# Residual and norm vectors loaded during the recurrence, query turns waiting bank by bank, in a two-block transformer kernel on one core

## The reference

```python
# block 1, MLA
q = (_rmsnorm(c_q, q_norm) @ w_uq).reshape(B, L, MLA_HEADS, MLA_QK_DIM)
q = jnp.concatenate([q[..., :MLA_NOPE_DIM], _rope(q[..., MLA_NOPE_DIM:], cos, sin)], axis=-1)
k = jnp.concatenate([k_nope, jnp.broadcast_to(k_rope, (B, L, MLA_HEADS, MLA_ROPE_DIM))], axis=-1)
mla = _block_sweep(q, k, mv, MLA_QK_DIM ** -0.5, key_end, mla_mask)
# block 2
...
x = layer_norm_affine(ALPHA * x + gt1 * mix_l, ln1_g, ln1_b)
h2 = modulate(layer_norm(x), sh2, sc2)
logits = jnp.einsum('btd,de->bte', h2, router_w)
ffn_l = expert_choice_ffn(h2, router_w, w_gate, w_up, w_down)
x = layer_norm_affine(ALPHA * x + gt2 * ffn_l, ln2_g, ln2_b)
```

## Time and profile before

| what | value |
|---|---|
| median of 3 runs | 1576.49 us (1571.98 to 1577.51) |
| the profiled execution, its own time | 1569.62 us |
| its span, first to last instruction | 1567.5 us |
| TensorE busy | 1427.5 us, 91% of the span, mean granted clock 0.959 |
| VectorE, ScalarE, GpSimd busy | 49%, 26%, 13% |
| DMA | 284.99 MB, mean 182 GB/s |
| chain that ended last | PE 75%, issue 10%, DVE 8%, ACT 2%, DMA 2%, POOL 2% |

### The profile page before, as it was taken

The page is one execution under the profiler, slowest core; times in us unless marked ns, Lnnn a source line. Parts: engine busy times, 40 slices in busy tenths (PEclk is TensorE's granted clock), DMA queues, the critical chain, the costliest instruction groups (busy, mean ns, idle before and its releaser), DMA issues.

```text
span 1567.5 us, 31894 instructions
## 1 busy us (share of the span) xinstructions
PE 1427.5 (91%) x14033; PEld 821.8 (52%) x14033; DVE 762.7 (49%) x1437; ACT 404.9 (26%) x902; POOL 206.6 (13%) x220
## 2 busy tenths in 40 slices
PE   7999999999999999969999997884999898998986
PEld 4546576764645556757888885352333332332322
DVE  5987455455236646656667765464132132122124
ACT  3220154632100025544555543011100000000002
POOL 1200013100001110033344362011000000000000
PEclk9999999999999998989999998895999999999998
DMA  7575321401401111000000000734999999999992
GB/s 283 194 255 195 142 107 31 149 1 41 176 27 54 54 54 55 1 2 4 5 4 4 4 4 26 326 126 176 394 428 426 427 427 429 427 426 429 428 428 102
DMA packets 50730, 284.99 MB, mean 182 GB/s; under 512 B 3992, under 2 KB 7320, under 8 KB 37792
## 3 DMA queue, kind: packets, MB, share of 16 engines
q1 hardware_dynamic: 46736, 267.20, 42.3%
q0 software_dynamic: 2704, 10.18, 1.9%
q10 hardware_dynamic: 1152, 5.57, 0.9%
HBM read 276.63 MB, written 6.29 MB: 180 GB/s over the span
## 4 chain that ended last, share of the span: by engine, by line
PE 75%; issue 10%; DVE 8%; ACT 2%; DMA 2%; POOL 2%; ACTq 0%; DVEq 0%; SPq 0%; POOLq 0%
PE PS L1319 15%; PE PS L1105 7%; PE PS L1339 7%; PE PS L723 7%; PE PS L1635 4%; PE PS L588 3%; PE PS L569 3%; PE PS L1123 3%; PE PS L553 3%; PE PS L1357 3%; PE PS L1702 2%; PE PS L691 2%; PE PS L685 2%; PE PS L759 2%; PE PS L547 2%
## 5 line engine op out<-in xcount | busy, mean ns | idle before, releaser
L1319 PE MATMUL PS<-arena 128*64 128x512 f32 x304 | 141.3, 615 | 14.9 <-issue 14.9
L1321 PE MATMUL PS<-arena 128*64 128x512 f32 x304 | 141.4, 615 | 0.0
L771 PE MATMUL PS<-arena,ring 128*128 128x512 f32 (+1 forms) x368 | 127.6, 508 | 0.0
L1319 PE MATMUL PS<-ring,arena 128*64 128x512 f32 x208 | 99.7, 630 | 12.5 <-issue 11.5
L723 PE MATMUL PS<-ring,arena 128*128 128x512 f32 (+1 forms) x256 | 109.1, 583 | 1.9 <-ACT arena L1769 1.9
L1105 PE MATMUL PS<-arena 64*64 64x64 f32 x3776 | 92.5, 224 | 9.5 <-DVE arena L1418 3.9
L771 PEld LDWEIGHTS PS<-arena,ring 128*128 128x128 f32 x368 | 69.4, 189 | 58.2 <-issue 54.3
L1321 PE MATMUL PS<-ring,arena 128*64 128x512 f32 x208 | 99.8, 631 | 0.0
L2479 DVE TENSOR_TENSOR arena<-PS,arena 64x512 f32<-64x512 f32 x32 | 22.1, 689 | 157.9 <-PE PS L1341 157.6
L645 DVE TENSOR_REDUCE arena<-PS 128x1 f32<-128x768 f32 (+4 forms) x96 | 62.7, 655 | 74.2 <-PE PS L553 25.5
L1319 PEld LDWEIGHTS PS<-arena 128*64 128x64 f32 x304 | 41.4, 141 | 101.7 <-issue 100.9
(11 more groups left out here) (382 smaller groups left out, 2683.3 us busy)
## 6 DMA issues: line engine op xcount, KB each, us to landing
arena<-exp_w_down SPq DMA_DIRECT2D x20, 2048.0 KB, 36.1
arena<-exp_w_gate SPq DMA_DIRECT2D x19, 2048.0 KB, 31.5
arena<-exp_w_up SPq DMA_DIRECT2D x19, 2048.0 KB, 35.7
ring<-exp_w_gate SPq DMA_DIRECT2D x13, 2048.0 KB, 29.6
ring<-exp_w_up SPq DMA_DIRECT2D x13, 2048.0 KB, 34.1
ring<-w_ada SPq DMA_DIRECT2D x12, 2048.0 KB, 12.8
ring<-exp_w_down SPq DMA_DIRECT2D x12, 2048.0 KB, 35.0
ring<-w_in SPq DMA_DIRECT2D x9, 2048.0 KB, 7.8
```

What stands on the lines that cost most here:

```text
L771: mm = pe.matmul(bank(b, 0, n), u[:, k, (i % 4) * P:(i % 4) * P + P], hT[:, k, t0:t0 + n], start=(k == 0), stop=(k == KT - 1))
L1319: pe.matmul(bank(c, 0, 512, (0, 64)), x, unit(u)[:, k, c * 512:c * 512 + 512], start=(n == 0 and k == 0), stop=(n == 1 and k == 3))
L1321: mm = pe.matmul(bank(c, 0, 512, (64, 128)), x, unit(u + 1)[:, k, c * 512:c * 512 + 512], start=(n == 0 and k == 0), stop=(n == 1 and k == 3))
```

## The change

The residual, `ln1` and the router are loaded by SP and no longer by ScalarE. SP issues `ln1` and the router when phase 6 (GQA) is over, and the residual when all operations of the recurrence have signalled, that is during RWPOST. The lives of the three tiles begin earlier accordingly. In MLAPREP each pair of heads waits only for the job slot in which its two banks lie (`q_bank`), and VectorE copies the odd heads, ScalarE the even ones.

```diff
-    ("x2", 4 * D, OUT2, FINAL), ("ln1", 2 * D, OUT2, ROUTE),
+    ("x2", 4 * D, RWPOST, FINAL), ("ln1", 2 * D, RWKV, ROUTE),
-    ("xn", 4 * D, OUT2, ROUTE), ("h2T", 2 * D, OUT2, ROUTE), ("router", 128, OUT2, ROUTE),
+    ("xn", 4 * D, OUT2, ROUTE), ("h2T", 2 * D, OUT2, ROUTE), ("router", 128, RWKV, ROUTE),

+SCAN_TOTAL = {}
+for _name, _n in SCAN_COUNT.values():
+    SCAN_TOTAL[_name] = max(_n, SCAN_TOTAL.get(_name, 0))

@@ SP @@
                 elif slot == SCAN_SLOT:
+                    sp.wait_ge(sem("phase_left"), 4 * 6)
+                    sp.dma_start(T("ln1"), w["ln1"].broadcast_to([P, 2 * D])).then_inc(sem("ln1_loaded"), 16)
+                    sp.dma_start(T("router"), w["router_w_2"][0].rearrange("(p k) e -> p k e", k=KT))\
+                        .then_inc(sem("ln1_loaded"), 16)
+                    for name, n in SCAN_TOTAL.items():
+                        sp.wait_ge(sem(name), n)
+                    sp.dma_start(T("x2"), x1_dram).then_inc(sem("x1_back"), 16)
                     sp.wait_ge(sem("phase_left"), 4 * 7)

@@ TensorE @@
+        def q_bank(h):
+            last_four = [n for n, j in enumerate(JOBS) if j[0] == MLAPREP][-4:]
+            return 2 * slot_of(last_four[h // 2]) + h % 2

-            for n in n0[-4:]:
-                e, c = emptied(n)
-                pe.wait_ge(sem("slot_dve" if e == "d" else "slot_act"), c)
             pe.wait_ge(sem("q_roped"), 4)
             for h in range(H):
+                if h % 2 == 0:
+                    n = n0[h // 2 - 4]
+                    e, c = emptied(n)
+                    pe.wait_ge(sem("slot_dve" if e == "d" else "slot_act"), c)
                 for t in range(4):
-                    mm = pe.transpose(bank(h, t * P, P, (0, QK)), qrow[:, t, h * QK:h * QK + QK], ident)
+                    mm = pe.transpose(bank(q_bank(h), t * P, P, (0, QK)), qrow[:, t, h * QK:h * QK + QK], ident)

@@ ScalarE @@
-            for h in range(H):
+            for h in range(0, H, 2):
                 act.wait_ge(sem("q_turned"), h + 1)
-                act.activation(mqT[0:QK, h, :], bank(h, 0, 512, (0, QK)), ACT.Copy, scale=MLA_SCALE)
+                act.activation(mqT[0:QK, h, :], bank(q_bank(h), 0, 512, (0, QK)), ACT.Copy, scale=MLA_SCALE)
...
-            act.dma_start(T("x2"), x1_dram).then_inc(sem("x1_back"), 16)
-            act.dma_start(T("ln1"), w["ln1"].broadcast_to([P, 2 * D])).then_inc(sem("ln1_loaded"), 16)
-            act.dma_start(T("router"), w["router_w_2"][0].rearrange("(p k) e -> p k e", k=KT))\
-                .then_inc(sem("ln1_loaded"), 16)

@@ VectorE @@
             jobs_empty(dve, "d", MLAPREP, rope_q)
+            for h in range(1, H, 2):
+                dve.wait_ge(sem("q_turned"), h + 1)
+                dve.tensor_scalar(mqT[0:QK, h, :], bank(q_bank(h), 0, 512, (0, QK)), MLA_SCALE, None, ALU.mult)
```

## The result

The changed kernel takes **1564.52 us**, the median of 7 runs (1559.30 to 1568.14). The kernel before, run beside it, takes 1575.24 (7 runs, 1569.37 to 1577.51). The ratio is 0.9935, with a 95% interval of 0.991 to 0.9959: 10.7 us faster by the medians, with an interval that leaves out 1. One execution of one kernel further down (`logits` later), 1867.87 us at a mean granted clock of 0.74 where all others have about 0.96, is left out of that kernel's ratio.

A forecast was written before the change was run, and what follows sets the result against it. TensorE, busy 91% of the span, was taken to bound the kernel. OUT2's 7.5 us plus the query turns' 2.0 us made 9.5 us, taking the 1576.49 us median to 1567.0, range 1560 to 1574.5.

The forecast's parts named there:

- OUT2, 7.5 us: Start of OUT2: TensorE's 5.64 us idle before the first turn goes, and 1.9 us returns through the clock.
- The upper bound of 8.7: OUT2: the most it could gain, the 8.7 us by which VectorE starts earlier.
- The time of issue moves too, and that carries the 7.5.: OUT2's three loads: issuing them earlier, when DMA engines are 2% and 1% busy, brings the 7.5 us.
- a mere move to SP would leave the wait where it is: OUT2's loads: changing only the issuing engine keeps the wait, leaving just the 2.0 us of the query turns.
- The residual as the case to reckon with: OUT2: the residual, 12.7 us in the crowd, would land at about 964, 28 us before VectorE needs it.
- The turns, 2.0 us: End of MLAPREP: earlier query turns and shared copies hand over at 279.0, not 280.98; bounds 0.9 to 2.6 us.
- What is late next: OUT2 after the change: TensorE no longer waits for VectorE's tile 1 and sets the pace to the end of `mixed(3)`.
- Addresses, nothing: Arena: the three tiles' longer lives move most tiles to other addresses, taken to cost nothing.
- The signs: Expected profile after: no idle before the first turn, residual near 962, `mixed(3)` done 9.5 us earlier, MLA's first matmul at 279.0.
- Rival A: OUT2: the idle goes but the clock stays low; 6.5 to 7.6 us gained, 1569 to 1570 us; chance 0.17.
- Rival B: OUT2's loads stay in the crowd or the expert stage gives the gain back; 1574.5 us; chance 0.08.
- Rival C: Recurrence: new loads hold up instruction fetches, 20.2 us cost, 10.7 us slower overall, 1587 us; chance 0.05.

The follow-up runs named there:

- `logits` later: Changed kernel with TensorE's logits(0) moved from ahead of mixed(3) to behind turn_xn(2); ratio to the kernel before 0.9934, run again 0.9923.
- the kernel with all copies on ScalarE: Changed kernel with ScalarE copying all eight query heads again, the bank-wise waits kept; ratio to the kernel before 0.9945.
- the kernel with eight loads: Changed kernel with the 1 MB load of `ln1` repeated seven more times during the recurrence; ratio to the kernel before 0.9941.
- the run with the vectors early: Changed kernel with the residual issued by ScalarE at OUT2's start again, only `ln1` and the router loaded early; ratio to the kernel before 0.9939.
- the addresses alone: Kernel before with only the longer lives of the three tiles, giving the changed kernel's arena addresses; ratio to the kernel before 0.9989.

## Why the prediction was right, and where its reasons were not

- **The time.** 1567.0 was predicted, 1564.5 measured, inside 1560.0 to 1574.5. The sum was 9.5 us, the two stages gained 10.66, inside its bounds of 6.5 and 11.3. Both parts moved by the mechanism that the sum names: TensorE's idle time and slow clock behind it in OUT2, and its wait for all four slots ahead of the turns.
- **OUT2, 7.5 us.** Measured 8.45 in the profile of after (7.6 to 8.8 over the profiles of kernels that leave the tail of OUT2 as it is). The parts, by the rows: the idle time 5.64 as said; the turn 1.97 - 0.87 = 1.10 as said; `mixed(2)` 14.64 - 13.74 = 0.90 for 0.8. Most of the rest, 0.77, is `mixed(0)` with `mixed(1)`, 29.81 for 30.58: the first 16 us of the stage were granted 0.87 after and 0.82 before, and the sum has no term for that. Whether it belongs to the change is open: the four profiles in which ScalarE still issues the residual there have 30.54 to 30.58, the others 29.43 to 30.09, but the kernel with all copies on ScalarE, whose loads are those of the changed kernel, has 30.66. The upper bound of 8.7 held in the profile of after; the kernel with eight loads, at 8.84, goes just past it.
- **"The time of issue moves too, and that carries the 7.5."** The early issue is enough for the gain, as the profile after shows, but this step took it for the cause, and it is not needed. Issued no earlier than before, but ahead of the expert units, the loads give the same OUT2 within the spread (105.76); behind them, 122.89. What the kernels that gain have in common is that all three loads have landed when `mixed(0)` is done; in the kernel before, `ln1` and the router came behind the residual, beside the expert units. The Trainium skill, "DMA: Bandwidth & Descriptors", section "Issuing engines are not separate DMA queues", says that transfers of all issuers run on the same 16 DMA engines and interleave. The runs agree: the residual takes 12.7 and 12.9 us on ScalarE beside the units, 7.7 alone. The conclusion that I drew from it, that a mere move to SP would leave the wait where it is, came out in neither place: the router lands after 24.3 us on ScalarE beside the units, 4.8 on SP ahead of them and 26.8 behind them.
- **The residual as the case to reckon with.** The working followed its 12.7 us. Early, it took 7.7 (the estimate, 12.7, was too long), and it did not need to be early at all: the run with the vectors early shows the gain with the residual left in the crowd.
- **The turns, 2.0 us.** Measured 2.21. VectorE's copy took 0.68 us for the 0.69 assumed. The hand-over came at 284.44 - 5.67 = 278.77 on the clock of before (5.67 is how much later the projection's row stands, 276.21 for 270.54), not at 279.0: the 0.2 us that I let pass between the last turn and its copy did not show, VectorE being still at head 5 until 283.68 when the last turn was over at 283.64. The path that I gave, last turn and then its copy, and VectorE's own path, its `mk` copies and then four copies back to back, end within 0.2 us of each other, and it was the second that set the end.
- **What is late next.** As said: TensorE, which runs from `mixed(0)` to the end of `mixed(3)` without a gap. `mixed(3)` ends 60.83 us after OUT2's start for 69.25 before, 8.42 earlier.
- **Addresses, nothing:** held in the two stages of the sum (6.66 and 113.94), and the ratio with the addresses alone cannot be told from 1. (Ahead of FOX the profile after loses 5.82 us, not the 4.6 that the expectation of that run names.)
- **The signs.** Those on waits and on the clock came as listed. Those in clock times (the residual near 962, `mixed(3)` 9.5 us before 1045.1, MLA's first matmul at 279.0, and wrong at 280 or later) cannot be read off the profile after, which stands 5.7 to 7 us later at these places, most of it from the way to FOX; the stages have to be compared instead. The 962 does not fit the working either, which has 964.
- **Rival A** (clock stays low): no, granted 1.00 in every window from 999 to 1044. **Rival B** (given back): no; from the end of OUT2 to the last matmul every profile takes 465.2 to 466.9 us, 465.27 before and 465.33 after. **Rival C** (instruction streams): no, eight loads cost nothing that shows. Its other side, a kernel that is slower, did come up in the experiments, by another mechanism: the place behind the experts, which I had not priced.

## What to carry to other kernels

A small load that a stage wants early should stand ahead of the bulk transfers: look for what was issued just before it on the same engine, how many MB that is and what the other engines issue at that moment, before looking for an idle stretch to hide it in. A wait is worth the idle time of the bound engine that it causes, and the clock that goes with it (here 5.64 + 2.0 us), not its own length (25.52 us). Where two profiles of nearly equal span hide a change, measure the stages between fixed instructions, and judge the change by those it can reach.

## What was unexpected

How far stages that no edit touches differ between kernels. The way to FOX takes 194.0 to 194.6 us in six profiles and 197.5 to 200.1 in seven others, among these both profiles of the changed kernel and those of the kernels with the turns alone and the loads alone. In all seven of the second group, and in none of the first, TensorE waits 2.1 to 3.0 us for VectorE at about 78 us, which is part of the difference, as in the timeline of the changed kernel run again:

```profile
78.54 7.11 PE L733 MATMUL PS<-ring,arena 128*128 128x512 f32 x16 [2.88 <-DVE arena L864]
```

In the kernel before there is no such wait at this place:

```profile
73.79 7.11 PE L723 MATMUL PS<-ring,arena 128*128 128x512 f32 x16
```

The recurrence, too, varies between 275.6 and 280.6 us, with no order by edit. GQA, whose instructions no edit touches, lies between 80.5 and 83.0. What sets any of these was not found; the first two together are as large as the gain, and they are why one profile against one could not have judged this change.
